# Squaring the residual rows in parts beside the last projection, and scaling them in quarters that the matrix engine turns at once

## The reference, cut to what matters

```python
merged = sigmoid(ga) * branch_a + sigmoid(gb) * branch_b
x = x + merged @ w_out                                  # the residual rows
xn = rmsnorm(x, g_ffn)                                  # x * rsqrt(mean(x*x) + eps) * g_ffn
q = xn @ w_q                                            # 8 heads, 2 x 128 columns each
s1, s2 = q[:, :, 0] @ keys1.T, q[:, :, 1] @ keys2.T     # 128 scores each
e, g = top 16 of the sums of top 16 x top 16, softmax   # 16 experts per head and token
act = gelu(sum_d u_tab[e] * xn);  x = x + sum_k (g * act) * v_tab[e]
y = rmsnorm(x, g_final)
```

## Time and profile before

| | |
|---|---|
| time, median of 3 runs | 3842.36 us (3833.04 to 3843.02) |
| the profiled execution's own time | 3830.24 us |
| its span | 3828.5 us |
| busy: PE, DVE, POOL, ACT | 3045.8, 2564.9, 1369.1, 675.3 us |
| chain that ended last: DMA, PE, DVE, issue | 39%, 26%, 19%, 11% of the span |
| `square_rows` to the first product with `w_q`, group A | 789.10 to 810.53 us |
| the same, group B | 1640.42 to 1674.07 us |

### The profile page before, as it was taken

How to read it: one execution, slowest core, us unless ns; L and a number is a source line. 1 busy time by engine, 2 the same in 40 slices (tenths; PEclk the granted TensorE clock), 3 DMA queues, 4 the chain that set the end, 5 groups by cost and what they waited for, 6 DMA issues and landing times.

```text
span 3828.5 us, 34630 instructions
## 1 busy us (share of the span) xinstructions
PE 3045.8 (80%) x11870; PEld 1932.7 (50%) x11870; DVE 2564.9 (67%) x3483; ACT 675.3 (18%) x1402; POOL 1369.1 (36%) x876
## 2 busy tenths in 40 slices
PE   6999989988999997979345455555178899999992
PEld 6999989976555554545211112222143344444441
DVE  3788830025777776757887888888875656665658
ACT  4444321011000000011000002555440000000000
POOL 2000000003333433323357676666512224434345
PEclk9999999989999998989767767887599999999996
DMA  4232267759999998988789999999859999999998
GB/s 123 87 87 86 85 188 240 237 192 347 356 383 379 370 387 314 384 304 319 273 360 421 422 422 420 417 421 401 327 189 360 369 414 421 421 421 421 421 422 352
DMA packets 389493, 1240.86 MB, mean 324 GB/s; under 512 B 22545, under 2 KB 263185, under 8 KB 263855
## 3 DMA queue, kind: packets, MB, share of 16 engines
q0 software_dynamic: 120720, 876.60, 56.5%
q1 hardware_dynamic: 258944, 356.03, 26.8%
q10 hardware_dynamic: 9711, 6.81, 0.6%
HBM read 1230.29 MB, written 9.90 MB: 324 GB/s over the span
## 4 chain that ended last, share of the span: by engine, by line
DMA 39%; PE 26%; DVE 19%; issue 11%; POOL 5%; ACT 1%; DVEq 0%; POOLq 0%; SPq 0%; ACTq 0%
DMA region<-in_v_tab_dram,region 29%; PE ps L1632 12%; DMA region<-in_u_tab_dram,region 7%; POOL region L610 5%; DVE region L1462 4%; DVE region L1406 4%; PE ps L1615 3%; PE ps L1617 3%; PE ps L1616 3%; DVE region L1397 2%; PE ps L1810 1%; DMA region<-in_w_q_dram 1%; DVE region L1343 1%; DVE region L1340 1%; DVE region L1342 1%
## 5 line engine op out<-in xcount | busy, mean ns | idle before, releaser
L610 POOL DMA_INDIRECT region<-in_u_tab_dram,region x544 | 861.6, 1584 | 1481.0 <-DVE region L1397 592.0
L1632 PE MATMUL ps<-region,region 128*128 128x160 f32 (+1 forms) x5120 | 1211.6, 400 | 72.2 <-DMA region<-in_w_q_dram 14.4
L1632 PEld LDWEIGHTS ps<-region,region 128*128 128x128 f32 x5120 | 853.9, 195 | 421.6 <-issue 41.8
L1462 DVE SCALAR_TENSOR_TENSOR region<-region,region 128x2048 f32<-128x2048 f32 x384 | 871.7, 2287 | 130.3 <-DMA region<-in_u_tab_dram,region 129.7
L1862 PE MATMUL ps<-region,region 128*128 128x512 f32 x2048 | 886.0, 594 | 33.7 <-DMA region<-in_v_tab_dram 32.9
L1406 DVE SCALAR_TENSOR_TENSOR region<-region,region,region 128x2048 f32<-128x2048 f32 x224 | 526.9, 2352 | 535.5 <-DMA region<-in_v_tab_dram,region 522.5
L1810 PE MATMUL ps<-region,region 128*128 128x512 f32 x512 | 362.3, 874 | 393.0 <-DMA region<-in_v_tab_dram,region 373.9
L1862 PEld LDWEIGHTS ps<-region,region 128*128 128x128 f32 x2048 | 387.9, 190 | 531.1 <-issue 479.0
L610 POOL DMA_INDIRECT region<-in_v_tab_dram,region x288 | 469.5, 1630 | 415.6 <-DVE region L1406 335.0
L1810 PEld LDWEIGHTS ps<-region,region 128*128 128x128 f32 x512 | 139.7, 286 | 600.5 <-issue 574.8
L1397 DVE SCALAR_TENSOR_TENSOR region<-region,region 128x2048 f32<-128x2048 f32 x160 | 363.0, 2285 | 17.5 <-DMA region<-in_u_tab_dram,region 17.3
(11 more groups left out here) (238 smaller groups left out, 1743.2 us busy)
## 6 DMA issues: line engine op xcount, KB each, us to landing
region<-in_v_tab_dram SPq DMA_DIRECT2D x128, 1024.0 KB
region<-in_w_in_dram SPq DMA_DIRECT2D x192, 512.0 KB
region<-in_w_out_dram SPq DMA_DIRECT2D x64, 512.0 KB
region<-in_w_q_dram SPq DMA_DIRECT2D x64, 512.0 KB
region<-in_w_a_dram SPq DMA_DIRECT2D x32, 512.0 KB
region<-in_w_b_dram SPq DMA_DIRECT2D x32, 512.0 KB
region<-in_u_tab_dram,region POOLq DMA_INDIRECT x544, 10.5
region<-in_x_prompt_dram SPq DMA_DIRECT2D x7, 1024.0 KB, 10.8
```

The costliest lines, as they stand in the source:

```text
L610: pool.indirect_dma_start(out=slot, out_offset=None, in_=rows_ap, in_offset=bass.IndirectOffsetOnAxis(ap=idx[:, k:k + 1], axis=0)).then_in ...
L1462: stt(out=u_b[s], in0=u_b[s], scalar=1.0, in1=xn_tile(UNITS_A + u), op0=ALU.mult, op1=ALU.mult, accum_out=dots[u % 2][:, k:k + 1]).then_in ...
L1632: last = mm(outs[n][:, 0:WIDTH[g]], wide[s][:, q, n * P:(n + 1) * P], rhs(k), start=(k == 0), stop=(k == n_k - 1))
```

## The change

Both groups are changed alike, and group B has an extra reordering.

- ACT squares the rows in three parts of columns: blocks 0 to 7, 8 to 13, and 14 and 15 (1024, 768 and 256 columns). The first part stands between two widenings of the last blocks (after block 11 in group A, after block 12 in group B), the others after all of them. Ahead of the first part stands a root of a constant, `root_ahead`. Each part has its own sum, and DVE adds the three sums of a row (`tensor_reduce`) before ACT takes the root.
- DVE scales in quarters of 512 columns, in the order 2, 3, 0, 1, and takes its odd blocks out of PSUM between the quarters. PE turns the four blocks of a quarter as soon as that quarter is scaled, so blocks come in the order 8 to 15, then 0 to 7.
- In group B, the blocks 0 to 7 go to a region that the gain also lies in, so ACT and DVE wait before those until all quarters are scaled.
- In group B, steps 123 to 125 stand behind the norm and the turning on DVE and on ACT.

```diff
+PARTS, SQUARES = (0, 8, 14, DC), (NT, NT + 7, NT + 17)
-            def square_rows(g):
+            def square_part(g, n):
+                first, end = PARTS[n:n + 2]
                 for j in range(2):
-                    act.wait_ge(x1_ready[j], CC * (g + 1) + 1)
-                for t in range(TILES[g].start, TILES[g].stop):
-                    act.wait_ge(ssq_ready, NT + t)
+                    act.wait_ge(x1_ready[j], CC * g + end // 2 + 1)
+                for t in range(g + 2):
+                    if t == 2:
+                        act.wait_ge(ssq_ready, SQUARES[1] + 3 * n + 1)
+                    part_sum, out = sums_x[g][:, t, n:n + 1], junk_n[g][t][:, first * P:end * P]
                     if g == 0:
-                        nc.scalar.activation(junk_n[0], xa[:, t, :], ACT.Square, accum_out=ssq[:, t:t + 1]).then_inc(ssq_ready, 1)
+                        ins = nc.scalar.activation(out, xa[:, t, first * P:end * P], ACT.Square, accum_out=part_sum)
...
+            def root_ahead():
+                nc.scalar.activation(small[:, 66:67], ones[:, 0:1], ACT.Sqrt)
+
+            def root_rows(g):
+                act.wait_ge(ssq_ready, SQUARES[g + 1])
                 nc.scalar.activation(rstd[:, TILES[g]], ssq[:, TILES[g]], ACT.Sqrt, bias=eps, scale=1.0 / D).then_inc(rms_sqrt, 1)
                 if g == 1:
                     for t in range(3):
                         act.dma_start(x1_d[t].rearrange("p (k n) -> p k n", n=P), xp[:, :, t * P:(t + 1) * P]).then_inc(x1_out, 16)
 
             def channels_out(g):
-                for k in range(0, DC, 2):
-                    act.wait_ge(xT_done, DC * (g + 1) + k + 1)
-                    nc.scalar.activation(xnt(g, k), bank(4 + k % 4)[:, 0:WIDTH[g]], ACT.Copy).then_inc(xT_act, 1)
+                for n in range(0, DC, 2):
+                    if g and n == CC:
+                        act.wait_ge(xn_ready, NT + 8 + 12)
+                    act.wait_ge(xT_done, DC * (g + 1) + n + 1)
+                    nc.scalar.activation(xnt(g, (n + CC) % DC), bank(4 + n % 4)[:, 0:WIDTH[g]], ACT.Copy).then_inc(xT_act, 1)
...
             for j in range(DC):
                 out_block(1, j)
                 expert_steps(*steps_out(j))
-            square_rows(1)
+                if j == 12:
+                    root_ahead()
+                    square_part(1, 0)
+            square_part(1, 1)
+            square_part(1, 2)
+            root_rows(1)
+            channels_out(1)
             expert_steps(*STEPS_NORM)
-            channels_out(1)
             expert_steps(*steps_query(0))
...
             def normalise_rows(g):
+                tiles = TILES[g]
+                dve.wait_ge(ssq_ready, SQUARES[g + 1] - 1)
+                nc.vector.tensor_reduce(ssq[:, tiles], sums_x[g], AX.X, ALU.add).then_inc(ssq_ready, 1)
                 dve.wait_ge(rms_sqrt, 2 + g)
-                link(nc.vector.reciprocal(rstd[:, TILES[g]], rstd[:, TILES[g]]))
+                link(nc.vector.reciprocal(rstd[:, tiles], rstd[:, tiles]))
                 dve.wait_ge(gffn_in, 16 * (g + 1))
...
+                for n, q in enumerate((2, 3, 0, 1)):
+                    if n >= 2:
+                        channels_out(g, 4 * n - 7, 4 * n - 3)
+                    cols, ks = slice(512 * q, 512 * q + 512), slice(4 * q, 4 * q + 4)
+                    for t in range(tiles.start, tiles.stop):
...
+                if g:
+                    dve.wait_ge(xn_ready, NT + 8 + 12)
+                channels_out(g, 9, DC)
...
-            expert_steps(*STEPS_NORM)
             normalise_rows(1)
-            channels_out(1)
+            expert_steps(*STEPS_NORM)
...
             def tokens_to_channels(g):
-                pe.wait_ge(xn_ready, NT + TILES[g].stop)
-                for k in range(DC):
-                    if k >= 4:
-                        pe.wait_ge(xT_dve if k % 2 else xT_act, DC + CC * g + (k - 4) // 2 + 1)
+                for n in range(DC):
+                    k = (n + CC) % DC
+                    if n % 4 == 0:
+                        pe.wait_ge(xn_ready, NT + 8 * g + (g + 2) * (n // 4 + 1))
+                    if n >= 4:
+                        pe.wait_ge(xT_dve if n % 2 else xT_act, DC + CC * g + (n - 4) // 2 + 1)
```

More of the change, by code:

```diff
@@ L259, in hybrid_step @@
         xnb = region(o_b, 3 * D).rearrange("p (t d) -> p t d", d=D)
-        junk_n = [region(3 * D, D), region(o_h, D)]
+        junk_n = [[region(o_u + t * D, D) for t in range(2)], [region(o_h + (t % 2) * D, D) for t in range(3)]]
         u_a = [region(at, D) for at in (o_w + 4 * PIECE, o_w + 6 * PIECE, o_u)]
@@ L348, in hybrid_step @@
         mask = small[:, 68:72]
+        sums_x = [small[:, 72:78].rearrange("p (t n) -> p t n", n=3), small[:, 78:87].rearrange("p (t n) -> p t n", n=3)]
         at2 = [0]
@@ L1033, in _ @@
                 out_block(0, j)
-            square_rows(0)
+                if j == 11:
+                    root_ahead()
+                    square_part(0, 0)
+            square_part(0, 1)
+            square_part(0, 2)
+            root_rows(0)
             channels_out(0)
@@ L1322, in channels_out @@
-            def channels_out(g):
-                for k in range(1, DC, 2):
-                    dve.wait_ge(xT_done, DC * (g + 1) + k + 1)
-                    nc.vector.tensor_copy(xnt(g, k), bank(4 + k % 4)[:, 0:WIDTH[g]]).then_inc(xT_dve, 1)
+                for n, q in enumerate((2, 3, 0, 1)):
[3 more added lines that the diff above has]
+                    for t in range(tiles.start, tiles.stop):
+                        if g == 0:
+                            stt(out=xna[:, t, cols], in0=xa[:, t, cols], scalar=rstd[:, t:t + 1], in1=gffn[0][:, cols],
+                                op0=ALU.mult, op1=ALU.mult).then_inc(xn_ready, 1)
+                        else:
+                            b = t - 2
+                            stt(out=xnb[:, b, cols].rearrange("p (k n) -> p k n", n=P), in0=xp[:, ks, b * P:(b + 1) * P],
+                                scalar=rstd[:, t:t + 1], in1=gffn[1][:, cols].rearrange("p (k n) -> p k n", n=P),
+                                op0=ALU.mult, op1=ALU.mult).then_inc(xn_ready, 1)
@@ L1327, in fifth_tile, with channels_out @@
+                if g:
+                    dve.wait_ge(xn_ready, NT + 8 + 12)
+                channels_out(g, 9, DC)
+            def channels_out(g, first, end):
+                for n in range(first, end, 2):
+                    dve.wait_ge(xT_done, DC + DC * g + n + 1)
+                    nc.vector.tensor_copy(xnt(g, (n + CC) % DC), bank(4 + n % 4)[:, 0:WIDTH[g]]).then_inc(xT_dve, 1)
             def fifth_tile(h):
@@ L1424, in _ @@
             normalise_rows(0)
-            channels_out(0)
             link(nc.vector.memset(sc_s, 0.0))
@@ L1572, in tokens_to_channels @@
             def tokens_to_channels(g):
[L1573 to L1576 removed]
+                for n in range(DC):
[4 more added lines that the diff above has]
+                        pe.wait_ge(xT_dve if n % 2 else xT_act, DC + CC * g + (n - 4) // 2 + 1)
                     if g == 0:
[L1578 to L1579 removed]
+                        tr(bank(4 + n % 4)[:, 0:P], xna[:, 0, k * P:(k + 1) * P], ident)
+                        last = tr(bank(4 + n % 4)[:, P:NA], xna[0:TS, 1, k * P:(k + 1) * P], ident[0:TS, 0:TS])
                     else:
                         for t in range(3):
[L1582 removed]
+                            last = tr(bank(4 + n % 4)[:, t * P:(t + 1) * P], xnb[:, t, k * P:(k + 1) * P], ident)
                     last.then_inc(xT_done, 1)
```

25 lines of the change are left out of this document (7 added, 18 removed).

## The result

The changed kernel takes 3814.84 us in the median of 11 executions (3805.34 to 3822.87); the kernel before, run beside it, 3833.04 us (3823.31 to 3843.86). The ratio is 0.9950 with a 95% interval of 0.9938 to 0.9961: faster by 19 us, with 15 to 24 us as the interval. The profiled execution has a span of 3813.0 us where before had 3828.5. The chain by engine (page, part 4) answers to the earlier trace rows: it is still one of transfers, with PE two points lower. A distance "behind the last widening" is counted throughout from the end of ACT's last copy of `w_out` products out of PSUM (line 880 in group A, line 883 in group B).

What follows compares the result with a forecast made beforehand. The bound changes by stage, with transfers holding 39% of the chain of waits. Group A's 6.35 us plus group B's 11.6 made 18.0 us, off the median 3842.36: 3824.4 us, own range 3812 to 3832, widened to 3808 to 3840.

Steps and rivals of the forecast that it cites:

- Group A, 6.35 us: Group A's norm: PE starts turning at 793.3 us instead of 799.65, a gain of 6.35 us, bounds 5.4 to 9.6.
- The table load, 1.3 us of A: Of the 3.2 us by which group A's scaling comes earlier, 1.3 are the table load, with no drain added.
- Group B up to the scaling: Group B's norm: scaling starts at 1644.1 us instead of 1658.05, and PE starts at 1646.3.
- The wait that takes over: Group B: ACT's copies wait behind its issue of the kept rows' three transfers, 7 us, leaving ACT free at 1650.6.
- Rival 1: Group B: issues take 17.8 us even without gathers, bound by their 2048 pieces each; 3835.2 us; chance 0.17.
- rival 2: Group B: issues take 1.9 us, so the quarters alone set the pace; 3823.0 us; chance 0.12.
- From release to product: Group B, ACT's release through copies, turning and last scaling quarter: 9.6 us; `w_q` starts at 1660.2, 13.9 us earlier.
- my own list: Would refute the forecast: kept rows' issue over 12 us, PE turning at another pace, end distance growing by what was won.
- The steps behind the turning: Group B: nine steps, not six, precede `route(9)`; DVE late by 2.3 us, 1706.3 instead of 1717.86, gain 11.6.
- Rival 3: Group B: nine expert steps become the bound, ending at 1734.9; loses 17.0 us there; 3853.0 us; chance 0.06.
- To the end: From `route(9)` to the kernel's end the distance should be as before, 2110 us.
- Rival 4: Group A's gain goes nowhere, since products with `w_q` wait for weights; 11.6 us remain, 3830.8 us; chance 0.05.

Runs made afterwards that it cites:

- A's half alone: Only group A changed, group B's squares, scaling and steps 123 to 125 in the old order; 3825.65 us, ratio 0.9979 to the kernel before.
- the kept rows behind: Changed kernel with the kept rows' three transfers issued behind ACT's last copy instead of ahead of its copies; 3815.04 us, ratio 0.9955 to the kernel before.
- B's half alone: Only group B changed, group A's squares and scaling in the old order; 3821.45 us, ratio 0.9966 to the kernel before.

## Why the prediction came out right, step by step

- **Base.** The forecast of 3824.4 us was 18.0 us below a median of three executions, 3842.36. Eleven executions give 3833.04 for the same kernel, and 3833.04 - 18.0 = 3815.0 against 3814.84. The error of the absolute time, 9.6 us, is that of the base. The forecast gain stands inside the measured interval. Measured against that high base, the time came only 2.8 us above the lower end of the forecast's own range (3812).
- **Group A, 6.35 us.** 6.8 by the distance, 8.0 (3.5 to 13) by the half alone. The parts were a little dear: two of 768 and two of 256 columns took 2.46 us (788.48 to 790.94), not 2.9, since they follow each other at 0.83 and 0.40 us without the 0.12 us that I added. The squares before waited for one another (`act.wait_ge(ssq_ready, NT + t)`); the change drops that wait. PE's start (1.5 us after the scaling), the pace and the clock (0.50 between 795 and 805 us, as before) were as predicted.
- **The table load, 1.3 us of A.** 1.1 by taking it out. In B it was worth nothing, which I had not seen. The rule of the Trainium skill (ScalarE: Activation LUTs, What ACT_TABLE_LOAD costs), a drain of 1380 ns beside the load, is not borne out: 0.01 us stand between load and root, and 1.1 us were won, not 2.7.
- **Group B up to the scaling.** 5.1 us predicted, 4.5 measured, again the parts (3.6 us for 4.3). The 25.48 us that I called PE's idle time are those of its weight loads; PE's own were 25.25, and nothing hangs on it.
- **The wait that takes over.** Predicted as ACT held by its own issue for about 7 us; it was held for 6.31, and its copy came 2.8 us later than PE's first block allows (1640.44 + 0.93, the distance with the kept rows behind, to 1644.13). That 7 and 6.3 agree is in part luck. I took the kept rows' drain as 296 GB/s, but that window holds the end of the drain: by single microseconds it went at 346 to 348 GB/s until 1668 and then ran out. In the changed kernel the engines moved nothing until 1639 and then 1.67 MB at 329 GB/s until the issue was over, so 1.2 us to begin and 5.1 of draining, where I had 2.3 and 4.7: two errors of opposite sign. The mechanism is shown by making it go (0.93 us to the copy) and by doubling it (9.0 us for 9.0 us). Rival 1, 17.8 us, and rival 2, 1.9 us, are out for this order. The sentence of the Trainium skill (DMA: Bandwidth & Descriptors, Issuing engines are not separate DMA queues), "usually small relative to the DMA itself", holds here for the first transfer, 0.62 us; the third took 3.91 us, where no transfer took more than 9.2 from issue to landing.
- **From release to product.** 9.6 predicted (the terms listed add up to 9.44), 8.9 measured. The term that was mis-sized is the turning of the last four blocks with the copy behind: 3.1 us forecast, 2.2 measured (1650.81 to 1653.01), because I kept the pace of before, when the clock was 0.50 until 1671, and here it was 1.00 from 1648. In B, then, PE did turn at another pace at the end, which my own list counts against the forecast; it moved the product by under a microsecond. The first product came 19.2 us behind the widening instead of 21.2: 0.6 from the parts, 0.7 from the issue, 0.7 here.
- **The steps behind the turning.** DVE is the late one by 1.9 us (2.3 predicted), and the value row of step 125 landed 12.9 us after the first dot product (13.1). From first product to `route(9)` are 45.6 us (46.1). `route(9)` came at 64.8 us instead of 67.3, so B gained 14.1 us where 11.6 were forecast: the step that was off is the sum of those small terms, each counted a few tenths too dear. Rival 3 is out.
- **To the end.** Predicted unchanged at 2110 us. It was 2114.4 in the one trace, 3.8 us more than before. The twelve traces are not without order here: the three kernels with the steps ahead had 2105.8 to 2110.6 us, the nine with the steps behind 2109.3 to 2116.5, in the mean 5.7 more. So a few microseconds of B's gain may be lost on the way to the end; not all, since B's half alone gave 13.0 us by its ratio for 13.8 at `route(9)`. The gains of the two places, 20.9 us, and the 19 of the whole agree within the interval, which leaves room for a loss of that size. No run settles it. Rival 4 is out by A's half alone, whose whole interval lies below 1.

What I had not seen is how B's gain is shared out. I had priced parts, quarters and steps in one chain. Undoing them singly costs 3.0, 1.0 and 15.6 us at `route(9)` (3.2, 0.9 and 17.4 at the first product), and of the last some 4.7 us are the hold, by the estimate above. The steps' place counts most; parts still serve B, since they let the issue begin earlier, and quarters hardly, since ACT's issue stands over the time that they win.

## What to carry to other kernels

Look at what an engine has to issue ahead of the instruction that others wait for: a transfer in its stream holds everything behind it for as long as its issue takes, and that length depends on what else the transfer engines have at that moment, not on the transfer alone. Once such a hold stands over a stretch, making the work beside it finer wins little (quarters: 0.9 us in B, 3.2 in A), while making shorter what stands ahead of it still pays (parts: 3.2 us in B). And ask what a new wait drags along: the sum of the parts on DVE tied ACT's issue to DVE's place in the steps. And read small gains as distances at the place, between two events that the edit can't touch, since the whole execution varies by more than they are.

## What the runs showed of the hardware

The issue of the same three transfers, 3.1 MB in 512-byte pieces, took ACT 5.8 to 6.6 us in the eight kernels in which no gather was under way as it began, 8.6 to 9.7 in the three in which steps or a dot had just freed some, and 17.8 us with three expert steps running beside it. Issued behind three others, the same three took 8.96 us for 3.1 MB, while the engines moved 331 GB/s. By single microseconds such stores drained at 295 to 350 GB/s with nothing beside them. What stood ahead of them in ACT's stream still ran during the issue (the root at 1647.80, in an issue row from 1646.53), what stood behind it did not: the next row of ACT came 0.04 to 0.09 us after its end in each of the ten traces in which that row was held. What sets the pace of that drain, the bytes or the 2048 pieces of each transfer, was not tried.
